# Neighbourhood attention: result scaled after the value product, and a reordered first projection

## What is computed

```python
hs = modulate(xs, g[0], ml[:, 0], ml[:, 1])             # rms_norm, then scale and shift per feature
rq, rk, rv, rg, nq, nk, nv = even_project(hs, w_in)      # one product with w_in_ac
s_loc = einsum(qg, kg) * scale + bias                    # a window of the grid, 32 columns of keys
s_ctx = einsum(qg, k_ctx) * scale                        # 128 context keys
p = softmax(concatenate([s_loc, s_ctx], -1))
o = einsum(p[..., :nloc], vg) + einsum(p[..., nloc:], v_ctx)
```

## Time and profile before

| | us |
|---|---|
| median of 3 runs | 1719.24 (1718.31 to 1721.92) |
| the profiled execution | 1718.75, its span 1716.6 |
| TensorE busy | 1658.2 |
| VectorE busy | 1078.6 |
| ScalarE busy | 731.9 |
| GpSimd busy | 198.7 |

### The profile page before, as it was taken

The page is one execution under the profiler, slowest core; times in us unless marked ns, Lnnn a source line. Parts: engine busy times, 40 slices in busy tenths (PEclk is TensorE's granted clock), DMA queues, the critical chain, the costliest instruction groups (busy, mean ns, idle before and its releaser), DMA issues.

```text
span 1716.6 us, 27096 instructions
## 1 busy us (share of the span) xinstructions
PE 1658.2 (97%) x10968; PEld 1508.5 (88%) x10968; DVE 1078.6 (63%) x1703; ACT 731.9 (43%) x1314; POOL 198.7 (12%) x195
## 2 busy tenths in 40 slices
PE   6999999899999999999999989999999999999998
PEld 4999878699999999999989974446999999999997
DVE  3777657947667687775687657875585643332344
ACT  3532326746643213223345756654475331221334
POOL 0000002423000000000220403433210000000011
PEclk9999998999999999999999999999999999999999
DMA  9455233033365465562321500003154622222231
GB/s 330 157 172 172 80 93 74 26 99 86 111 210 167 127 176 164 152 196 74 105 47 41 157 7 1 1 1 98 38 153 141 198 74 74 74 74 75 78 95 62
DMA packets 266606, 182.86 MB, mean 107 GB/s; under 512 B 26302, under 2 KB 238131, under 8 KB 265459
## 3 DMA queue, kind: packets, MB, share of 16 engines
q1 hardware_dynamic: 266410, 180.87, 36.0%
q10 hardware_dynamic: 72, 0.26, 0.0%
HBM read 173.88 MB, written 4.67 MB: 104 GB/s over the span
## 4 chain that ended last, share of the span: by engine, by line
PE 79%; DVE 10%; ACT 5%; issue 3%; DMA 2%; SPq 1%; POOL 1%; DVEq 0%; ACTq 0%; POOLq 0%
PE ps L863 21%; PE ps L865 21%; PE ps L864 21%; PE ps L1531 3%; PE ps L1541 2%; DMA ada_a<-in_w_ada 1%; DVE w_lo L581 1%; ACT w_hi L572 1%; PE ps L917 1%; PE ps L1117 1%; ACT km L2072 1%; PE ps L1119 1%; PE ps L1118 1%; DVE sq L2811 1%; DVE w_lo L2779 1%
## 5 line engine op out<-in xcount | busy, mean ns | idle before, releaser
L572 ACT ACTIVATE w_hi<-stage 128x1024 fp32r<-128x1024 f32 (+1 forms) x176 | 184.8, 1052 | 608.4 <-PE ps L865 513.6
L581 DVE TENSOR_TENSOR w_lo<-stage,w_hi 128x1024 fp32r<-128x1024 f32 (+1 forms) x175 | 215.7, 1234 | 280.6 <-ACT w_hi L572 280.4
L863 PE MATMUL ps<-hM_hi,w_lo 128*128 128x320 f32 x952 | 296.0, 311 | 0.0
L864 PE MATMUL ps<-hM_lo,w_hi 128*128 128x320 f32 x952 | 294.5, 309 | 0.0
L865 PE MATMUL ps<-hM_hi,w_hi 128*128 128x320 f32 x952 | 294.5, 309 | 0.0
L863 PE MATMUL ps<-h_hi,w_lo 128*128 128x320 f32 x824 | 256.4, 311 | 2.8 <-DVE h_lo L2655 2.6
L865 PE MATMUL ps<-h_hi,w_hi 128*128 128x320 f32 x824 | 254.6, 309 | 0.0
L864 PE MATMUL ps<-h_lo,w_hi 128*128 128x320 f32 x824 | 254.6, 309 | 0.0
L2906 POOL TENSOR_TENSOR rstd<-rstd,sq 128x320 f32<-128x320 f32 x73 | 77.0, 1060 | 966.4 <-ACT sq L1616 964.7
L863 PEld LDWEIGHTS ps<-hM_hi,w_lo 128*128 128x128 f32 x952 | 179.1, 188 | 3.6 <-issue 3.5
L864 PEld LDWEIGHTS ps<-hM_lo,w_hi 128*128 128x128 f32 x952 | 179.2, 188 | 0.2 <-issue 0.2
(11 more groups left out here) (446 smaller groups left out, 3491.1 us busy)
## 6 DMA issues: line engine op xcount, KB each, us to landing
stage<-in_w_mlp_out SPq DMA_DIRECT2D x83, 512.0 KB, 4.3
stage<-in_w_mlp_in SPq DMA_DIRECT2D x80, 512.0 KB, 4.2
slab_mlp<-in_w_ada SPq DMA_DIRECT2D x28, 1024.0 KB, 5.3
stage<-in_w_in_ac SPq DMA_DIRECT2D x28, 512.0 KB, 3.9
slab_ac<-in_w_ada SPq DMA_DIRECT2D x12, 1024.0 KB, 6.2
ada_a<-in_w_ada SPq DMA_DIRECT2D x8, 1024.0 KB, 16.9
stage<-in_w_out_ac SPq DMA_DIRECT2D x8, 512.0 KB, 4.3
stage<-in_w_out_c SPq DMA_DIRECT2D x8, 512.0 KB, 4.3
```

Source lines behind the costliest of these rows:

```text
L572: nc.scalar.activation(hi_place(n)[:, 0:width], stage[:, n % STAGE, 0:width], ACT.Copy)\
L581: nc.vector.tensor_tensor(lo_place(n)[:, 0:width], stage[:, n % STAGE, 0:width], hi_place(n)[:, 0:width].bitcast(F32), ALU.subtract).then_ ...
L863: mm(out, lo[:, k], xh, start=j == 0, stop=False)
L864: mm(out, hi[:, k], xl, start=False, stop=False)
```

## The change

In the neighbourhood attention, VectorE no longer multiplies the weights by the inverse sums. It takes both heads' reciprocals in one instruction (into `inverse_sums(t)`), TensorE spreads them over the 64 rows of each head by two products with the identity into the last quarter of the result's bank, and VectorE copies the result and multiplies it by them. The transposes wait for the exponentials. `gn_blocks` gives two blocks a step over ten steps where it gave three over seven, and `high_at` and GpSimd's `low_after` are moved to suit. In the beginning, unit 0 runs k = 0, 1, 2 alone, then unit 1, then both; the wait for weights is per unit; 28 idle transposes stand for 26; the prompt's transposes go from ahead of k = 2 to ahead of k = 4, the spread of the norms from ahead of k = 6 to k = 7. The second half's odd tiles of the first norm are scaled on VectorE. ScalarE splits pieces 4 and 5 after unit 2 rather than after unit 0.

```diff
-AFFINE_NO = {"in0": 0, "in0m": 1, "in1m": 2}
+AFFINE_AT = {("in0", k): k // 2 for k in range(0, KD, 2)}
+AFFINE_AT.update({(name, k): KD // 2 + KD * n + k for n, name in enumerate(("in0m", "in1m")) for k in range(KD)})
...
         def gn_blocks(t):
-            return [divmod(n, 5) for n in range(3 * (t - 2), 3 * (t - 1)) if 0 <= n < 5 * PAIRS]
+            return [divmod(n, 5) for n in range(2 * (t - 2), 2 * (t - 1)) if 0 <= n < 5 * PAIRS]
+
+        def inverse_sums(t):
+            return smA[:, 2 + t // 3 % 2, 2 * (t % 3):2 * (t % 3) + 2]
...
             def units_beside(units, part, beside=None):
-                pe.wait_ge(w_lo_done, units[-1] + 1)
+                alone = 3 if units == (0, 1) else 0
                 together = KD - 2 if part else KD
-                steps = [(k, units) for k in range(together)]
+                steps = [(k, (g,)) for g in units for k in range(alone)]
+                steps += [(k, units) for k in range(alone, together)]
...
                     for g in at_once:
+                        if k == 0:
+                            pe.wait_ge(w_lo_done, g + 1)
...
-            keep_running(26)
+            keep_running(28)
...
-            units_beside((0, 1), 0, {2: turn_prompt, 6: lambda: spread_rows(1)})
+            units_beside((0, 1), 0, {(4, 0): turn_prompt, (7, 0): lambda: spread_rows(1)})
...
             def na_turn(t):
                 for e in range(2):
-                    pe.wait_ge(na_p, 2 * t + e + 1)
+                    pe.wait_ge(na_e, 2 * t + e + 1)
...
             def na_values(t):
...
+                pe.wait_ge(na_p, t + 1)
+                for e in range(2):
+                    last = mm(ps[64 * e:64 * e + 64, 6 + t % 2, 3 * P:4 * P],
+                              inverse_sums(t)[:, e:e + 1].to_broadcast([P, HD]), ident[:], start=True, stop=True)
...
-                if name not in AFFINE_NO:
+                if (name, k) not in AFFINE_AT:
...
-                if k == 4:
+                if k == 6:
                     for j in range(8, 10):
                         act.wait_ge(x_t, j + 1)
...
             for j in range(20):
-                if j == 1 or j > 3:
-                    act_split(act, 5 if j == 1 else j + 2)
+                if j > 3:
+                    act_split(act, j + 2)
...
-                if j == 0:
+                if j == 2:
                     act_split(act, 4)
+                    act_split(act, 5)
...
                 if t >= 3:
                     act.wait_ge(na_t, 2 * (t - 3) + e + 1)
+                    act.wait_ge(na_p, t - 2)
...
-            high_at = {9: 0, 10: 1, 12: 2, 14: 3, 15: 4, 17: 5, 21: 6}
+            high_at = {9: 0, 11: 1, 14: 2, 16: 3, 17: 4, 18: 5, 21: 6}
...
-                if k == 4:
+                if k == 5:
                     token_roots(1)
...
-            def na_norm(t, e):
-                w, x = 384 if t % 5 < NB else TC, 2 * (t % 3) + e
-                dve.wait_ge(na_e, 2 * t + e + 1)
-                link(nc.vector.reciprocal(smA[:, 2, x:x + 1], smA[:, 1, x:x + 1]))
-                ts(pA[:, x, 0:w], pA[:, x, 0:w], smA[:, 2, x:x + 1], None, ALU.mult).then_inc(na_p, 1)
+            def na_norm(t):
+                x = 2 * (t % 3)
+                dve.wait_ge(na_e, 2 * t + 2)
+                nc.vector.reciprocal(inverse_sums(t), smA[:, 1, x:x + 2]).then_inc(na_p, 1)
...
             def na_store(t):
                 m, b = divmod(t, NB + 1)
                 dve.wait_ge(na_pv, t + 1)
+                result = oT[:, 4 + m, P * b:P * (b + 1)]
+                link(nc.vector.tensor_copy(result, ps[:, 6 + t % 2, 0:P]))
...
-                nc.vector.tensor_copy(oT[:, 4 + m, P * b:P * (b + 1)], ps[:, 6 + t % 2, 0:P]).then_inc(na_out, 1)
+                tt(result, result, ps[:, 6 + t % 2, 3 * P:4 * P], ALU.mult).then_inc(na_out, 1)
...
-            low_after = {7: (0,), 8: (1,), 9: (2,), 10: (3,), 11: (4, 5, 6, 7)}
+            low_after = {7: (0,), 8: (1,), 9: (2,), 11: (3, 4, 5, 6, 7)}
```

More of the change, by code:

```diff
@@ L889, in units_beside @@
             def units_beside(units, part, beside=None):
-                pe.wait_ge(w_lo_done, units[-1] + 1)
+                alone = 3 if units == (0, 1) else 0
                 together = KD - 2 if part else KD
-                steps = [(k, units) for k in range(together)]
+                steps = [(k, (g,)) for g in units for k in range(alone)]
+                steps += [(k, units) for k in range(alone, together)]
                 steps += [(k, (g,)) for g in units for k in range(together, KD)]
                 for k, at_once in steps:
-                    if beside and k in beside:
-                        beside[k]()
+                    if beside and (k, at_once[0]) in beside:
+                        beside[k, at_once[0]]()
                     h_ready("in0", part)(k, k)
                     for g in at_once:
+                        if k == 0:
+                            pe.wait_ge(w_lo_done, g + 1)
                         hi, lo = [w.rearrange("p (k m) -> p k m", k=KD)[:, k] for w in (hi_place(g), lo_place(g))]
@@ L1644, in operand @@
                 last.then_inc(affine_done, 1)
-                act.wait_ge(affine_done, KD * AFFINE_NO[name] + k + 1)
+                act.wait_ge(affine_done, AFFINE_AT[name, k] + 1)
                 f(out[:, k, half(1)], place, ACT.Copy).then_inc(h_hi_done[1], 1)
@@ L2215, in modulate @@
                     last = stt(place, x, coef[:, layer, which, k, 0:1], spread(name, 0), ALU.mult, ALU.mult)
-                elif name not in AFFINE_NO:
+                elif (name, k) not in AFFINE_AT:
                     for a, b, g in HALVES[1]:
@@ L2563, in _ @@
                         na_rowmin(t, e)
-                for e in range(2):
-                    if t <= N_NA:
-                        na_norm(t - 1, e)
+                if t <= N_NA:
+                    na_norm(t - 1)
                 if t == 3:
```

## The result

The changed kernel takes **1711.88 us** in the median of 4 runs (1710.79 to 1712.24), beside 1720.58 for the kernel before in as many (1718.31 to 1723.4): ratio 0.995, 95% interval 0.9933 to 0.9967. The forecast was 1711.8. The profiled execution took 1712.16 us, its span 1710.4: 6.2 less than before.

The account below looks back on a forecast made before the run. TensorE, busy 97% of the span, was taken to bound the kernel, so only its idle time or work pays. From 1718.75 us, 3.4 (beginning) and 3.6 (attention) were subtracted, giving 1711.75, say 1711.8; range 1708.0 to 1716.5.

Parts of the forecast that it names:

- The attention, 3.6 us: Neighbourhood attention: TensorE's idle 9.2 us less 4.4 and 0.2 for added products and 1.0 of remaining waits gains 3.6 us.
- the one before it, at half speed: Attention: one step with added products falls before the clock is back at 293.65 us, delaying the full-speed stretch by 0.2.
- the products 3.4, forecast 4.6: Attention: the added TensorE rows, four a step, cost 4.4 us over 19 full-clock steps plus 0.2, together 4.6.
- the 9.2 us of idle time: Attention at full clock: TensorE's idle time that can be won, taken as 9.2 us between 8.2 and 10.2.
- The slower rival: Attention: value products wait for the result's copy and multiplication, idle time stays, the beginning gives nothing; 1723.4 us, chance 0.03.
- The beginning, 3.4 us: First 75 us: unit 4 starts 2.9 us sooner with the clock lowered or 3.9 with it kept; 3.4 taken.
- The pass of units 0 and 1 ends 0.3 us sooner: Beginning, first projection: with the clock lowered until 44.28 us as before, the early products end this pass 0.3 us sooner.
- Moving the prompt's transposes and the spread costs neither time nor a wait: Beginning, units 0 and 1: these are the same work a little later, so the move costs 0 us.
- The chain takes some 11.3 us: Beginning, second half's tiles: four odd tiles save 4 x 0.6 us on ScalarE, leaving a chain of 11.3 us.
- It just fits; that cover is 0.2 us thin: Beginning, unit 4: piece 4's low part is ready at 72.2 or 71.1 us, wanted at 72.35 or 71.35.
- the order itself, taken for a gain at either clock: Beginning: running steps alone early ends the pass of units 0 and 1 0.3 us sooner, or 1.3 with the clock kept.
- more comes: Rival: clock kept in the beginning, no attention wait left, or a later half-speed stretch missed; 1709.3 us, chance 0.12.

Follow-up runs that it names:

- order-undone kernel: Changed kernel with the old order of steps for units 0 and 1 (no step alone), the new waits kept; median 1709.92 us, ratio 0.9935 to the kernel before.
- before again: The kernel before, unchanged, profiled a second time; it and the changed kernel's second profile are given as 1722.13 and 1713.38 us.
- beginning alone: Kernel before with only the beginning's part of the change, the attention as before; median 1716.38 us, ratio 0.9979.
- The early split: Changed kernel with VectorE's split of piece 4 placed ahead of the last five `w_ada` sums before it; median 1710.22 us, ratio 0.9946 to the kernel before.
- attention alone: Kernel before with only the attention's part of the change, the beginning as before; median 1710.41 us, ratio 0.9939.
- splits alone: Kernel before with only ScalarE's splits of pieces 4 and 5 moved behind the copy of unit 2; median 1717.79 us, ratio 0.9992.
- doubled spread: Changed kernel with the two products that spread the inverse sums done twice in each block; median 1714.80 us, ratio 0.9968 to the kernel before.

## Why the prediction was right, and which steps were not

**The attention, 3.6 us: right at an equal half-speed stretch (4.0), 2.4 in the profile.** Compared under equal half-speed stretches, old and new attention differ by 4.0 us twice. At 10.2 us the order-undone kernel's is 4.03 ahead of the kernel before's. At 13.7 us the old one loses 1.54 to 1.63 (before again, beginning alone) and the new one gains 2.42 to 2.47 (five profiles), 4.0 apart. In the profiled run the stretch was one length longer, which took 1.6 of it. The step that failed is "the one before it, at half speed": it took the stretch of before for the new one's. Its terms: waits of 1.3 us left, forecast 1.0; the products 3.4, forecast 4.6. With these two the sum would give 9.2 - 3.4 - 1.3 = 4.5, so some 0.5 of the 9.2 us of idle time was not there to be won. The slower rival, value products that wait for the store, has no wait in any profile of the new attention.

**The beginning, 3.4 us: wrong, 1.2.** Four steps failed against the lower end of 2.9. Of the 1.7 us that are missing there, the fourth unit lost 0.93 and unit 4 the rest.
- "The pass of units 0 and 1 ends 0.3 us sooner": it ended 0.35 later. I let the half speed end at 44.28 as before, so that its start lay in the wait ahead of 41.15. It began 1.14 us later, at 42.04, and so fell almost wholly into products. The three products at full speed ahead of it gained nothing, as TensorE waited for tile 2 behind them. This is 0.65 of the fourth unit's 0.93; of the rest, 0.2 is that the last tiles gave back 0.6 us and not 0.8.
- "Moving the prompt's transposes and the spread costs neither time nor a wait": the second half's first product waits for the spread, which came at 49.86 and not at 48.62, and so the tiles began 1.04 us later than before.
- "The chain takes some 11.3 us": it took 12.1, from 51.28 to the end of the last low part at 63.4; forecast was 61.6. A pair of tiles took 2.4 us and not 2.1, and ScalarE waited 1.45 us at 60.64 behind VectorE's split of a weight, 1.22 us, which the count for VectorE left out. TensorE did not wait for these tiles; what comes later for them is the sums of `w_ada` and the low part of piece 4. No run takes this step or the one before it alone; both are read from the trace.
- "It just fits; that cover is 0.2 us thin": it did not. The low part of piece 4 was ready at 73.98, 1.8 us later than forecast by the two steps above, and unit 4 lost 0.8 us. The early split took just that back. The thinness was named and still costed at nothing.

And the order itself, taken for a gain at either clock, is a loss of 0.8 us at full clock beside the old order with the same waits.

**Behind 339 us: not in the sum.** 2.6 us came there: 1.5 from the missing half speed at 894, 0.75 at 965, 0.4 from the `w_lo` wait near 602, which goes with the old attention. The rival "more comes" named the first at 0.12. These 2.6 us brought 3.6 (1.19 and 2.43) to 6.2. Set against the forecast's 7.0, the total came near 1711.8 by errors that cancel, which is luck. The line gives the changed kernel 7.0 ± 0.7 at equal clock and the attention alone 6.4 ± 0.7, of which the traces place 4.0 in the attention and 0.4 near 602 us, and 0.75 more at 965 us if that belongs to the change: it was lost in three of the four profiles with the old attention and in none with the new. Where the rest lies stays open.

## What to carry to other kernels

Before a loop is reordered so that a unit runs alone, ask for each step which operand comes last: here the order that waits for the later of two lost 0.8 us, though its first product came just as early. Before work is moved to a later place as costing nothing, ask who waits for its result. Where a cover is thinner than the errors of the terms it is made of, cost half of what it hides. And where stretches of half clock come and go, compare kernels from landmark to landmark under equal stretches, since one profile's total can be right for the wrong reasons.

## What the runs showed of the hardware

The granted clock fell or stayed behind the same code and waits. Behind 2.68 us idle at 41 us it fell in both profiles of before, and stayed with the attention alone and with the splits alone. Behind some 0.26 and then 1.85 us idle it fell in five profiles, at 41 to 44 us, and stayed in that of the doubled spread. It fell behind idle pieces of 0.19 to 0.63 us too. The stretch of 6.8 us near 1004 us was missing in two profiles, the beginning alone's and the splits alone's, and they gained 1.4 to 1.5 us there. In runs of the kernel before alone the mean clock went from 0.984 to 0.994 and the span from 1724.0 to 1711.6 us; that is more than this change is worth. A half-speed stretch of 3.4 us cost 1.5 us in the beginning and 1.2 to 1.6 at the attention's start. One at 333 us, with the splits moved alone and the old attention, whose TensorE still had idle time to give, cost 0.1.
